# One trunk layer on one core: rows transposed unscaled, index queries in three rounded passes, the norm multiplied in behind them, and attention's two ends rearranged

## What is computed

```python
def split_projection(h, w_in):
    ...
    qa, ka, va, qb, kb, vb, iq, ik, iw, ga, gb = jnp.split(jnp.dot(h, w_in), IN_SPLITS, axis=-1)

def dsa_attention(q, iq, iw, qpos, k, v, ik, kpos, bias_tab, topk):
    dots = jnp.einsum('bqhd,bsd->bqhs', iq, ik, ...) * IDX_SCALE
    score = jnp.einsum('bqh,bqhs->bqs', iw * IDX_HEAD_SCALE, jax.nn.relu(dots))
    ...
    _, sel = lax.top_k(score, topk)
    # softmax attention over the selected keys

# per layer: h = rmsnorm(x, g_attn); branches; merged = sig(ga) * (oa @ w_branch_a) + sig(gb) * (ob @ w_branch_b)
x = x + jnp.dot(merged, w_out)
x = x + moe_ffn(rmsnorm(x, g_ffn), ...)
gate = jax.nn.sigmoid(jnp.dot(rmsnorm(x, g_ple), w_ple_gate))
return x + gate * jnp.dot(p_i, w_ple)
```

## Time and profile before

| | |
|---|---|
| median of 3 runs | 1035.34 us (1034.95 to 1037.19) |
| profiled execution: its time | 1036.8 us |
| profiled execution: span | 1035.0 us |
| mean granted clock of PE | 0.967 |
| busy: PE / PEld | 925.9 / 591.2 us |
| busy: DVE / ACT / POOL | 378.2 / 256.5 / 132.4 us |

### The profile page before, as it was taken

One profiled execution on the slowest core, in us unless ns is written; L12 is line 12 of the kernel. 1 busy time (PEld: TensorE's weight loads), 2 busy tenths in 40 slices (PEclk: granted clock), 3 DMA queues, 4 the chain that ended last, 5 costly groups with the idle time before them and its releaser, 6 DMA issues.

```text
span 1035.0 us, 14155 instructions
## 1 busy us (share of the span) xinstructions
PE 925.9 (89%) x5699; PEld 591.2 (57%) x5702; DVE 378.2 (37%) x974; ACT 256.5 (25%) x523; POOL 132.4 (13%) x136
## 2 busy tenths in 40 slices
...
GB/s 265 118 152 2 203 1 62 1 2 68 263 105 120 78 46 244 128 236 239 427 427 425 427 428 428 424 428 425 429 426 426 427 426 425 427 428 264 254 22 66
DMA packets 60132, 263.72 MB, mean 255 GB/s; under 512 B 11054, under 2 KB 36030, under 8 KB 46224
## 3 DMA queue, kind: packets, MB, share of 16 engines
...
## 4 chain that ended last, share of the span: by engine, by line
PE 63%; DMA 29%; DVE 4%; ACT 2%; issue 1%; SPq 1%; DVEq 0%; ACTq 0%
DMA arena<-in_w_up 25%; PE ps L1111 13%; PE ps L1278 12%; PE ps L980 5%; PE ps L1143 4%; PE ps L1426 4%; PE ps L1303 3%; PE ps L881 3%; PE ps L952 3%; DMA arena<-in_w_ple 2%; PE ps L1044 2%; PE ps L1014 2%; PE ps L1065 2%; PE ps L1399 1%; PE ps L1172 1%
## 5 line engine op out<-in xcount | busy, mean ns | idle before, releaser
L1278 PE MATMUL ps<-arena,hT 128*64 128x512 f32 x960 | 234.5, 641 | 39.4 <-DMA arena<-in_w_up 39.2
L1278 PEld LDWEIGHTS ps<-arena,hT 128*64 128x64 f32 x960 | 71.6, 141 | 199.3 <-issue 149.4
L2211 DVE TENSOR_TENSOR xf<-xf,ps 128x256 f32<-128x256 f32 x32 | 13.5, 421 | 401.6 <-ACT xf L1699 379.1
L1111 PE MATMUL ps<-arena_merge,arena_merge 128*128 128x256 f32 x624 | 99.7, 287 | 0.0
L1303 PE MATMUL ps<-arena,xf 128*64 128x512 f32 x336 | 76.7, 598 | 12.8 <-DVE xf L2214 12.8
L1111 PEld LDWEIGHTS ps<-arena_merge,arena_merge 128*128 128x128 f32 x624 | 87.4, 188 | 0.0
L836 POOL DMA_INDIRECT expert_rows<-xf,arena x32 | 32.2, 1007 | 425.6 <-ACT xf L1703 399.8
L1111 PE MATMUL ps<-xf_merge,arena_merge 128*128 128x256 f32 x480 | 82.0, 288 | 0.0
L1699 ACT ACTIVATE xf<-ps 128x256 f32<-128x256 f32 x30 | 11.6, 385 | 259.1 <-PE ps L1278 259.1
L1111 PEld LDWEIGHTS ps<-xf_merge,arena_merge 128*128 128x128 f32 x480 | 69.3, 188 | 0.0
L1703 ACT ACTIVATE xf<-ps 128x512 f32<-128x512 f32 x30 | 17.9, 598 | 159.8 <-PE ps L1303 159.8
...
## 6 DMA issues: line engine op xcount, KB each, us to landing
...
arena<-in_w_in SPq DMA_DIRECT2D x3, 2048.0 KB, 10.5
...
```

The costliest lines, as they stand in the source:

```text
L1111: mm = pe.matmul(w[:, 2 * lo_t:lo_t + hi_t], rounded(st[:, c, cols]), rounded(mv[:, c, lo_t:hi_t]), start=c == 0 and k == 0, stop=c == pla ...
L1278: mm = pe.matmul(ps[g * BLK:(g + 1) * BLK, 2 + s, :], xsT[:, c, col:col + BLK], expert_columns(k, slice(0, 2), c, g), start=c == 0, stop=c ...
```

## The change

1. **Front.** The five tiles are transposed as they land (`x_nat` in place of `xf`); the DVE's eviction still multiplies by g_attn, whose load is now counted with the first tile (`x_in[0]`, 32), also for ACT's first square. The loads of the other two gains go behind the constants. The root is made for all five tiles at once, behind the five evictions.
2. **Keys first.** `slab_ikw` is loaded before `slab[0]`. PE projects the index keys from the unscaled `hT`; the DVE multiplies the root in as it evicts them. POOL spreads the root over a diagonal (two instructions), a matmul with ones turns it into a row repeated on all partitions ('rstd', a new use of WIDE).
3. **Index queries** from the unscaled `hT` in three rounded passes. ACT makes eight high halves (`raw_hi`, arena_front_86) and four of the weights (`iq_hi`, arena_front_82 and _83). The low halves: chunks 0 to 3 by POOL, 4 to 7 by the DVE (both into arena_merge_77), those of the weights by POOL, in place in `slab[0]` (arena_front_78).
4. **Norm behind.** Once the low halves are made, the DVE multiplies `hT` by the spread root (eight instructions), ACT makes the high halves `hT_f` from that, and POOL, after iq 3 has been projected, the low ones in the place of the raw ones. The low half of `slab_kvb` still follows on POOL.
5. **Order on PE.** keys, root, iq 0, table, iq 1, key transposes, iq 2, iq 3, dots; 8 warm-up matmuls in place of 24.
6. **Attention's start.** Window biases are built before the selection for 's'; `SELECT_FIRST` 6 and 11 entries in `SELECT_AT`, nine of them in branch A. The last query projection (now qa 3; the order is 0, 2, 1, 3) is made at u = 1, behind the first scores, with turns 0 and 1 behind it; ACT evicts it at u = 4.
7. **Attention's end.** The first gate is made ahead of the last weighing (at the last turn) by the general `three`, with its weights' low halves made by POOL during attention (behind the sets that end with units 23 and 31). `load_chunk(1)` waits for the last row maximum instead of the last output copy; ACT's gates don't wait for it any more.

```diff
+QA_ORDER = [0, 2, 1, 3]
 WIDE, WIDE_DONE = ring(
-    [(('xT', t), 'dve') for t in range(TILES)] + [(('iq', m), 'dve') for m in range(4)]
-    + [(('ikT', s), 'dve') for s in 'ps']
+    [(('xT', t), 'dve') for t in range(TILES)] + [('rstd', 'dve'), (('iq', 0), 'dve'), (('iq', 1), 'dve')]
+    + [(('ikT', s), 'dve') for s in 'ps'] + [(('iq', 2), 'dve'), (('iq', 3), 'dve')]
...
-SELECT_FIRST = 10
-SELECT_AT = [9, 17, 25, UNITS_A + 1, UNITS_A + 4, UNITS_A + 7, UNITS_A + 10]
+SELECT_FIRST = 6
+SELECT_AT = [6, 9, 12, 15, 18, 21, 24, 27, 30, UNITS_A + 1, UNITS_A + 4]
...
+        raw_low(0)
+        raw_low(1)
+        pool.wait_ge(rstd_ready, 1)
+        pool.tensor_tensor(rstd_of[:, 0:NP]..., ident..., nrm[:, 0:4]..., ALU.mult)
+        pool.tensor_scalar(rstd_of[:, NP:NT], ident[:, 0:NS], nrm[:, 4:5], None, ALU.mult).then_inc(rstd_spread, 1)
+        raw_low(2)
+        raw_low(3)
+        for m in range(4):
+            pool.wait_ge(sw_high, m + 1)
+            low_of(slab[0][:, :, m * P:(m + 1) * P], ..., iq_hi[m], "front").then_inc(sw_split, 1)
+        pool.wait_ge(wide_full, WIDE[('iq', 3)].fill)
         for c in range(KD):
-            pool.wait_ge(f_high, c + 1)
+            pool.wait_ge(f_high, KD + c + 1)
             low_of(hT_lo[:, c, :], hT[:, c, 0:NT], hT_f[:, c, :]).then_inc(f_split, 1)
...
-                mm = pe.transpose(w[:, c, 0:r], xf[0:r, t, c:D:KD], ident[0:r, 0:r])
+                mm = pe.transpose(w[:, c, 0:r], x_nat[0:r, t, c:D:KD], ident[0:r, 0:r])
...
+        def index_queries(m):
+            w = wide(open_slot(WIDE, ('iq', m), wide_out))
+            pe.wait_ge(f_high, KD)
+            pe.wait_ge(sw_high, m + 1)
+            for k in range(3):
+                if k == 1:
+                    pe.wait_ge(f_split, KD // 2)
+                    pe.wait_ge(raw_split, KD // 2)
+                if k == 2:
+                    pe.wait_ge(sw_split, m + 1)
+                for c in range(KD):
+                    st = slab[0][:, c, m * P:(m + 1) * P] if k == 2 else iq_hi[m][:, c, :]
+                    mv = raw_lo if k == 1 else raw_hi
...
-        act.wait_ge(f_split, KD)
+        act.wait_ge(f_split, KD // 2 + KD)
...
+        for c in range(KD // 2, KD):
+            dve.wait_ge(f_high, c + 1)
+            dve.tensor_tensor(rounded(raw_lo[:, c, :]), hT[:, c, 0:NT], ...raw_hi[:, c, :]..., ALU.subtract).then_inc(raw_split, 1)
+        dve.wait_ge(f_split, KD // 2)
+        dve.wait_ge(raw_split, KD // 2)
+        w = wide(close(WIDE, 'rstd', wide_full))
+        for c in range(KD):
+            ins = dve.tensor_tensor(hT[:, c, 0:NT], hT[:, c, 0:NT], w[:, 0:NT], ALU.mult).then_inc(hn_ready, 1)
...
         for u in range(len(UNITS) + WEIGH):
+            if u == 1:
+                project_queries('qa', QA_ORDER[-1], 7)
+                turn(0)
+                turn(1)
...
+            if LAG + 2 <= u < len(UNITS) + LAG:
+                turn(u - LAG)
+            if u == len(UNITS) + LAG - 1:
+                pe.wait_ge(max_ready, len(UNITS))
+                first_gate().then_inc(late_full, 1)
```

317 lines of the change are left out of this document (177 added, 140 removed).

## The result

The changed kernel takes 1055.13 us (median of 4 runs, 1051.63 to 1057.97) against 1035.21: a ratio of 1.0187, 95% interval 1.0158 to 1.0215. It is slower by 19.9 us; 18.2 were forecast. The profiled execution took 1053.72 us, its span 1051.9 at a mean granted clock of 0.959, 16.9 more than the one of before. Four more runs in another series gave 1055.76 (1052.78 to 1058.18).

A forecast was written before the change was run, and what follows sets the result against it. PE work was taken to bound the kernel until about 590 us, then weight traffic. Terms 16.8 + 0.6 + 2.2 - 1.4 = +18.2 us gave 1053.5 against the median 1035.34; range 1036.5 to 1060.

The forecast's parts named there:

- The bound and the carry-over: Whole kernel: PE work queues until weight traffic from about 590 us; gains or losses in the first 395 us arrive 1:1.
- POOL's low halves behind the last query: Front: POOL makes normed low halves only after the last query, so the first relu comes 10.5 us behind it.
- Turns: Front: DVE and POOL alternate whole instructions when both read two SBUF operands; 2.6, 6.7 and 4.5 us lost at three places.
- two signs of being wrong: Front: the forecast is wrong if raw low halves take 0.65 us each, or PE doesn't wait inside query 0.
- Fewer warm-ups: Front: fewer warm-up matmuls cost nothing, since PE waits for rows anyhow.
- The landing: Front: g_attn, issued at 3.13 us, lands 6.1 later, at 9.2.
- Attention's start: Moved query projection: scores start earlier, but units behind wait; net +0.6 us, or 0 to -1 if the clock stays up.
- Nine rounds in branch A: Attention's first half: nine selection rounds on the DVE in place of three cost +2.2 us, bounds 0 and +4.
- The end: Attention's end: first gate ahead of the last weighing, its weights' low half on POOL; -1.4 us, bounds -2 and -1.
- The faster case: Rival for the whole kernel: last query projected before 51.8 us, about -4 in all, 1031 us; chance 0.12.

The follow-up runs named there:

- a_again: The changed kernel run once more, unchanged, for a second trace and its scatter: 1055.76 us (1052.78 to 1058.18).
- e2: e1 plus index query 3 reading the raw low halves first, so POOL may overwrite them earlier: 1044.19 us, 1.0085 of the kernel before.
- v0: Kernel before with the changed front's cheap half: unscaled rows, plain fp32 index queries, no raw halves, attention as before but for query projection order: 1036.18 us against 1035.95.
- s_select_back: Changed kernel with selection rounds as before, 10 ahead of attention and 7 within: 1056.26 us, 1.0222 of the kernel before.
- e3: Changed kernel with POOL spreading the root before making its raw low halves: 1052.32 us, 1.0157 of the kernel before.
- e1: Changed kernel with POOL making the key/value slab's low half ahead of its wait for index query 3: 1047.24 us, 1.0132 of the kernel before.
- g_gate_back: Changed kernel with the first gate back behind the last output copy, its low halves still on POOL: 1055.97 us, 1.0208 of the kernel before.
- f2: v0 plus the changed end of attention and empty matmuls at attention's start and before the first index query: 1029.76 us against the kernel before's 1035.71.
- f1: Kernel before with 13 empty matmuls on PE at attention's start: 1032.19 us against 1035.71, ratio 0.9963.

## Why the prediction was right, and where it was not

**The bound and the carry-over** held: what was lost up to 400 us, 18.0, arrived as 16.9 in the span, within what the weight transfers vary. That the 18.0 lies so near the forecast 18.2 is luck in part: the front lost less than forecast, attention's start more, and in a_again 21.3 had been lost at the same place.

**POOL's low halves behind the last query** were the main step, and they came out as worked out: 10.5 from the last query to the first relu (10.48 measured), shown by e2, and by v0, where the cover is back and the wait gone. In s_select_back PE lost nothing inside query 0 and the relu was still 10.1 later than before, so this step doesn't lean on the turns inside the query. That raw and normed low halves share one place, and that the scores take the place of `hT`, could be read in the code and the order alone.

**Turns** came out too. Expected were 2.6 lost by the root, 6.7 inside query 0, 4.5 at the first weighing. The root lost 2.15, and all of it goes in e3. The weighing lost 3.7, and all of it goes in e1. Inside query 0 PE waited for 2.24 only (by the prediction's own times, 29.7 and 36.6, it was 6.9). That term was mis-sized through a neighbour: I had the keys end at 26.6, at a full clock, and they ended at 30.3, since PE had stood 2.4 us for the root's eviction and its clock fell to 0.54. The raw halves were ready at 37.0, where I had 36.6. That is luck in part: the DVE began them 3.4 later than forecast, and they took 6.3 instead of 9.3, since POOL was half through with its own. e3, in which the keys keep their clock, shows the 7.0 of idle time that I had expected. The two sizes, 6.7 of waiting and 3.7 of slow keys, are not to be added: they are one wait, seen from two sides. For the queries behind the wait I had 28.0 with 2.2 for a low clock. The first trace took 26.6, and a_again, e1 and e2, whose clock fell there, 28.1. The prediction named two signs of being wrong, raw halves at 0.65 each and no wait inside query 0. Both came in s_select_back, whose second weighing was still 13.9 later than before; they judge the turns and not the sum.

**Fewer warm-ups** were put at nothing, and that term failed. In the eight traces with 8 warm-up matmuls the root starts 6.95 to 8.14 us behind the landing of g_attn, after transposes at a low clock; in the three with 16 or 18 it is 6.66. So 0.3 to 1.5 us go there. The landing, forecast for 9.2, came at 9.7 to 11.0.

The Trainium skill, page "SBUF — State Buffer", section "SBUF: two separate sides", on which two of the three items had leaned, holds here at sizes that rows 7 did not cover: instructions of 128x5 (0.17 to 1.22 us), a weighing with three operands (0.49 to 4.21), and the four copies of 32x2 (5.02 in all beside POOL, 0.66 before). The DVE's subtractions with PSUM as a source kept their 1.46 us for two beside POOL (64.96) as without (44.16), which I had only assumed.

**Attention's start** was mis-sized: +0.6 forecast, +2.2 measured. I had allowed 0 to -1 for a clock that stays up, and 0.6 for one as before. It fell twice, within the moved projection and again at the 256-wide scores. The 10.0 us that I had from the first to the 256-wide scores came as 9.9 with the clock up (e1) and as 11.4 with it down. Even with the clock up the start lost 0.7 (102.7 against 102.0 from the second weighing), where I had allowed 0 to -1.

**Nine rounds in branch A**: +2.2 forecast, +2.0 measured, with both kernels slowed by the clock there. With the clock up in both it is 3.0 (44.9 against 41.9). That fits the prediction, by which three of the rounds are hidden in PE's slow stretch, but it isn't the rounds' price alone: the two kernels differ there in the late eviction and turns too, and s_select_back gave 1.8 back. The early rounds were worth their price all the same (s_select_back).

**The end**: -1.4 forecast, -1.6 measured, and by g_gate_back it is the gate's place. Low halves on POOL within attention cost nothing: 41.9 from the 256-wide scores to the weighing of values with them (f2) and without (f1).

**The faster case** needed a first relu before 62. v0 and f2 reach 62.0 and 60.3, without rounded queries.

**The range**, 1036.5 to 1060, held the time; both series' medians lie 1.6 and 2.3 above the 1053.5, and the single runs spread over 6.6 us. By the traces, what moves them is at two places up to 400 us, the first 45 us and attention's start.

**Open** is what decides in a given run whether the clock falls at attention's start: the kernel before may have kept it in three runs of a series of 17 (1028.61 to 1028.91, the others 1034.37 to 1038.22), but there is no trace of such a run. What decides whether the DVE or POOL goes first at the raw halves is open too.
